# An expert's up product as seven half-size products, with the weight sums on VectorE

## The reference, cut to what matters

```python
N_EXPERTS = 8
TOP_K = 2
D_FF_EXPERT = 3584
...
    def one(args):
        xb, e = args
        return (jax.nn.silu(xb @ w_gate[e]) * (xb @ w_up[e])) @ w_down[e]
```

## Time and profile before

| what | value |
|---|---|
| median of 3 runs | 3447.71 us (3436.28 to 3449.22) |
| the profiled execution | 3443.41 us, span 3441.6 us |
| TensorE matmuls | 3270.9 us busy, 95% |
| VectorE | 895.5 us busy, 26% |
| ScalarE | 690.6 us busy, 20% |
| GpSimd | 494.8 us busy, 14% |
| mean granted TensorE clock | 0.963 of 2.4 GHz |

### The profile page before, as it was taken

One profiled execution on the slowest core, in us unless ns is written; L12 is line 12 of the kernel. 1 busy time (PEld: TensorE's weight loads), 2 busy tenths in 40 slices (PEclk: granted clock), 3 DMA queues, 4 the chain that ended last, 5 costly groups with the idle time before them and its releaser, 6 DMA issues.

```text
span 3441.6 us, 81881 instructions
## 1 busy us (share of the span) xinstructions
PE 3270.9 (95%) x35194; PEld 2864.1 (83%) x35195; DVE 895.5 (26%) x1990; ACT 690.6 (20%) x1505; POOL 494.8 (14%) x441
## 2 busy tenths in 40 slices
PE   7999789999999999999999999989999999999998
PEld 5886678888887788787799887778899999988888
DVE  2324745553223321114233114131000110011001
ACT  2324132221113422212211021201111211100011
POOL 1210125555221010100057010000000000000000
PEclk9999689999899999999999999989999999999999
DMA  6546012222233244343344443238999999944477
GB/s 275 197 165 233 3 49 86 85 85 86 74 104 110 96 149 141 128 138 107 110 160 159 158 135 109 88 132 336 376 381 400 387 395 380 399 153 147 140 274 292
DMA packets 94204, 638.90 MB, mean 186 GB/s; under 512 B 10720, under 2 KB 11760, under 8 KB 36480
## 3 DMA queue, kind: packets, MB, share of 16 engines
q1 hardware_dynamic: 91472, 628.62, 49.0%
q0 software_dynamic: 2608, 8.49, 0.8%
HBM read 636.02 MB, written 1.05 MB: 185 GB/s over the span
## 4 chain that ended last, share of the span: by engine, by line
PE 88%; DMA 4%; DVE 3%; issue 2%; ACT 2%; POOL 1%; SPq 0%; ACTq 0%; DVEq 0%; POOLq 0%
PE bank L1109 18%; PE bank L663 17%; PE bank L618 12%; PE bank L781 12%; PE bank L802 5%; PE bank L634 5%; PE bank L719 3%; PE bank L1069 2%; DMA ring<-in_moe_down 2%; PE bank L566 2%; DMA ring<-in_moe_up 1%; PE bank L592 1%; PE bank L1124 1%; PE bank L838 1%; PE bank L820 1%
## 5 line engine op out<-in xcount | busy, mean ns | idle before, releaser
L781 PE MATMUL bank<-PROJ,ring 128*64 128x80 f32 (+1 forms) x7424 | 484.6, 257 | 10.8 <-DMA ring<-in_moe_down 6.6
L1109 PE MATMUL bank<-MIX,ring 128*64 128x80 f32 x12544 | 471.9, 234 | 18.3 <-issue 7.5
L781 PEld LDWEIGHTS bank<-PROJ,ring 128*64 128x64 f32 (+1 forms) x7424 | 441.7, 145 | 52.4 <-DMA ring<-in_moe_down 11.8
L1109 PEld LDWEIGHTS bank<-MIX,ring 128*64 128x64 f32 x12544 | 447.0, 137 | 44.1 <-issue 37.0
L618 PE MATMUL bank<-H,ring 128*128 128x256 f32 x1856 | 407.3, 382 | 4.3 <-ACT H L1297 4.3
L618 PEld LDWEIGHTS bank<-H,ring 128*128 128x128 f32 x1856 | 354.3, 191 | 56.8 <-issue 4.7
L1109 PE MATMUL bank<-H,ring 128*128 128x256 f32 x896 | 195.3, 381 | 0.0
L1109 PEld LDWEIGHTS bank<-H,ring 128*128 128x128 f32 x896 | 171.3, 191 | 23.9 <-issue 0.3
L663 PE MATMUL bank<-H,ring 128*64 128x128 f32 (+1 forms) x1296 | 184.8, 330 | 5.8 <-ACT H L1297 5.1
L663 PE MATMUL bank<-MIX,ring 128*64 128x128 f32 (+1 forms) x1272 | 181.1, 321 | 0.8 <-DVE MIX L1884 0.8
L802 PE MATMUL bank<-H,ring 128*128 128x256 f32 x768 | 178.1, 390 | 3.9 <-ACT PROJ L1396 3.7
(11 more groups left out here) (383 smaller groups left out, 3716.8 us busy)
## 6 DMA issues: line engine op xcount, KB each, us to landing
ring<-in_moe_up SPq DMA_DIRECT2D x224, 1024.0 KB, 7.2
ring<-in_moe_down SPq DMA_DIRECT2D x128, 896.0 KB, 6.3
ring<-in_up SPq DMA_DIRECT2D x44, 1024.0 KB, 4.8
ring<-in_mod_b SPq DMA_DIRECT2D x40, 1024.0 KB, 4.9
ring<-in_tproj SPq DMA_DIRECT2D x32, 1024.0 KB, 4.8
ring<-in_proj SPq DMA_DIRECT2D x26, 1024.0 KB, 4.8
ring<-in_gates SPq DMA_DIRECT2D x24, 1024.0 KB, 4.8
ring<-in_swup SPq DMA_DIRECT2D x22, 1024.0 KB, 4.8
```

Source lines behind the costliest of these rows:

```text
L781: mm = pe.matmul(B[bank][lo:lo + m, 0:width], w[:, k, lo:lo + m], src(s * half + k), start=s == 0 and k == 0, stop=s == 1 and k == half - 1)
L1109: mm = pe.matmul(B[(t0 + 2 * j + t) % 4][lo:lo + m, 0:n], w[:, k, t * P + lo:t * P + lo + m], src[:, k, 0:n], start=k == 0, stop=k == KT - 1)
```

## The change

The dense branch takes `up_seven`, `gate_seven` and `expert_seven` in place of `up` and the two `swiglu`. The sparse branch keeps its code and adds to the new semaphores what the dense branch would have. The four weight sums of a unit run on VectorE; GpSimd has no part in it.

```diff
+        def e_x(b, s):
+            return H[:, 4 * b:4 * b + 4, s * P:(s + 1) * P]
+        def e_x_sum(i):
+            return MIX[:, 4 + i, :].rearrange("p (k t) -> p k t", t=P)
+        def e_parts(j):
+            at = T + P * (j % 2)
+            return X[:, 0:4, at:at + P], X[:, 4:6, at:at + P]
+        def e_banks(j):
+            b0 = 4 * (j % 2)
+            return b0, [b0 + 1 + i for i in range(3)]
...
+                def up_seven(e):
+                    with pe.Fori(0, ET // NSLOT) as it:
+                        for j in range(NSLOT):
...
+                            pe.wait_ge(S("sv_c"), e * ET + it * NSLOT + (RES_E + j - 1))
+                            if j == 1:
+                                pe.wait_ge(S("mo_wc"), e + 1)
+                            product(w_quarter(u, 0, 0), e_x(0, 0), solo, 0).then_inc(S("sv_p1"), 1)
+                            product(w_quarter(u, 0, 1), e_x(1, 0), pair[0], 0)
+                            pe.wait_ge(S("e_s"), e * ET + it * NSLOT + (j + 1))
+                            if j == 0:
+                                pe.wait_ge(S("sv_x"), e * 4 + (X_E + 4))
+                            product(w_sum(u, j, 1), e_x_sum(1), pair[0], 1).then_inc(S("sv_p"), 1)
+                            product(w_sum(u, j, 0), e_x_sum(0), pair[1], 0)
+                            product(w_sum(u, j, 2), e_x_sum(2), pair[1], 1).then_inc(S("sv_p"), 1)
+                            product(w_sum(u, j, 3), e_x(1, 1), pair[2], 0)
+                            product(w_quarter(u, 1, 1), e_x_sum(3), pair[2], 1).then_inc(unit_done, 1)
+                    pe.wait_ge(S("sv_c"), e * ET + (RES_E + ET))
...
-                        up(e, H, T)
+                        up_seven(e)
                     with pe.Else():
                         pe.sem_inc(S("mo_w"), 1)
+                        pe.sem_inc(S("sv_p1"), ET)
+                        pe.sem_inc(S("sv_p"), 2 * ET)
                         up(e, XG, CAP)
...
+            def gate_seven(e):
+                        act.wait_ge(S("sv_p1"), e * ET + it * NSLOT + (RES_E + j + 1))
+                        act.activation(part[:, 1, :], B[e_banks(j)[0]][:, 0:P], ACT.Copy).then_inc(S("sv_c0"), 1)
+                        act.wait_ge(S("sv_c"), e * ET + it * NSLOT + (RES_E + j + 1))
...
+                        act.activation(CONV[:, j % 2, 0, 0:T].rearrange("p (s t) -> p s t", t=P), d[:, 0:2, :], ACT.Silu)\
+                           .then_inc(S("sw_s"), 1)
...
+            def expert_seven(e):
...
+                def w_sums(j, it):
...
+                    dve.tensor_tensor(s2, a11, a21, ALU.subtract).then_inc(S("e_w"), 1)
...
+                    dve.tensor_tensor(s0, a21, a22, ALU.add).then_inc(S("e_w"), 1)
...
+                    dve.tensor_tensor(s1, s0, a11, ALU.subtract).then_inc(S("e_w"), 1)
...
+                    dve.tensor_tensor(s3, a12, s1, ALU.subtract).then_inc(S("e_s"), 1)
...
+                def unit(j, it, ahead):
...
+                    dve.tensor_tensor(d[:, 1:3, :], d[:, 1:3, :], both[2], ALU.add).then_inc(S("sv_c"), 1)
+                    if ahead:
+                        w_sums(j + 2, it)
+                    dve.wait_ge(S("sw_s"), e * ET + it * NSLOT + (FT + j + 1))
+                    g = CONV[:, j % 2, 0, 0:T]
+                    dve.tensor_tensor(g, g, GW[:, :], ALU.mult).then_inc(S("moe_g"), 1)
...
+                w_sums(0, 0)
+                dve.wait_ge(S("mo_xg"), e * 2 + 2)
+                dve.tensor_tensor(t1, x12, x11, ALU.subtract).then_inc(done, 1)
+                dve.tensor_tensor(t3, x22, x12, ALU.subtract).then_inc(done, 1)
+                dve.wait_ge(done, e * 4 + (X_E + 2))
+                dve.tensor_tensor(t2, x22, t1, ALU.subtract).then_inc(done, 1)
+                dve.wait_ge(done, e * 4 + (X_E + 3))
+                dve.tensor_tensor(t4, x21, t2, ALU.subtract).then_inc(done, 1)
+                w_sums(1, 0)
+                with dve.Fori(0, ET // NSLOT - 1) as it:
+                    for j in range(NSLOT):
+                        unit(j, it, True)
...
```

More of the change, by code:

```diff
@@ L472, in seven_parts @@
             return d.rearrange("p (i t) -> p i t", t=n), e.rearrange("p (i t) -> p i t", t=n)
+        RES_E = sum(4 if s in DOWNS else SEVEN_UNITS[s] for s in SEVEN)
+        X_E = sum(12 if s in DOWNS else 4 for s in SEVEN)
+        def e_x(b, s):
[8 more added lines that the diff above has]
+            return b0, [b0 + 1 + i for i in range(3)]
         def hid(width):
@@ L1111, in up, with product @@
                             mm.then_inc(unit_done, 1)
+                def up_seven(e):
+                    with pe.Fori(0, ET // NSLOT) as it:
+                        for j in range(NSLOT):
+                            u = MOE0 + j
+                            solo, pair = e_banks(j)
+                            def product(left, right, bank, half):
+                                for k in range(4):
+                                    for lo, m in strips(P):
+                                        mm = pe.matmul(B[bank][lo:lo + m, half * P:(half + 1) * P], left[:, k, lo:lo + m], right[:, k, :],
+                                                       start=k == 0, stop=k == 3)
+                                return mm
+                            pe.wait_ge(slot_full[slot_of(u)], e * (16 * PER_E // NSLOT) + it * 16 + 16 * (u // NSLOT + 1))
+                            pe.wait_ge(S("sv_c"), e * ET + it * NSLOT + (RES_E + j - 1))
[12 more added lines that the diff above has]
+                    pe.wait_ge(S("sv_c"), e * ET + (RES_E + ET))
                 def down(e, hidden, n):
@@ L1528, in swiglu @@
                     pair(j, 0)
+            def gate_seven(e):
+                t0 = tile_base["moe_up"]
+                with act.Fori(0, ET // NSLOT) as it:
+                    for j in range(NSLOT):
+                        d, part = e_parts(j)
+                        act.wait_ge(S("sv_p1"), e * ET + it * NSLOT + (RES_E + j + 1))
+                        act.activation(part[:, 1, :], B[e_banks(j)[0]][:, 0:P], ACT.Copy).then_inc(S("sv_c0"), 1)
+                        act.wait_ge(S("sv_c"), e * ET + it * NSLOT + (RES_E + j + 1))
+                        act.wait_ge(lin_free, it * (2 * NSLOT) + (t0 + 2 * j + 2) + e * (2 * ET + KT))
+                        act.activation(CONV[:, j % 2, 0, 0:T].rearrange("p (s t) -> p s t", t=P), d[:, 0:2, :], ACT.Silu)\
+                           .then_inc(S("sw_s"), 1)
             act.wait_ge(S("first_in"), 16)
@@ L1655, in _ @@
                 with act.If(dense):
-                    swiglu("moe_up", T, e)
+                    gate_seven(e)
                 with act.Else():
+                    act.sem_inc(S("sv_c0"), ET)
                     swiglu("moe_up", CAP, e)
@@ L2109, in pair @@
                     g = CONV[:, j % 2, 0, 0:width]
-                    if e is not None and width == T:
-                        dve.wait_ge(S("mo_wc"), e + 1)
-                        dve.tensor_tensor(g, g, GW[:, :], ALU.mult).then_inc(S("moe_g"), 1)
-                        dve.wait_ge(S("moe_g"), it * NSLOT + (j + 1) + es)
                     dve.tensor_tensor(PROJ[:, bass.ds(it * (NSLOT * width) + j * width, width)], g,
@@ L2249, in _ @@
                     dve.tensor_copy(GW[:, :], B[5][:, T:TC]).then_inc(S("mo_wc"), 1)
-                    swiglu("moe_up", FT, T, e)
+                    expert_seven(e)
                     add_down(MOE0 + ET, e)
@@ L2256, in _ @@
                     dve.sem_inc(S("moe_g"), ET)
+                    dve.sem_inc(S("e_w"), 3 * ET)
+                    dve.sem_inc(S("e_s"), ET)
+                    dve.sem_inc(S("sv_x"), 4)
+                    dve.sem_inc(S("sv_k"), 3 * ET)
+                    dve.sem_inc(S("sv_c"), ET)
                     for i in range(4):
```

34 lines of the change are left out of this document (added).

## The result

| | before | after |
|---|---|---|
| median of the runs, us | 3445.53 (3436.28 to 3449.22, 4 runs) | 3546.27 (3536.25 to 3552.25, 4 runs) |
| profiled run: span, us | 3441.6 | 3544.2 |
| mean granted clock of TensorE | 0.963 | 0.948 |

The ratio is 1.0287, with a 95% interval of 1.0272 to 1.0301: **slower by 2.9%**, where 0.5% faster was forecast. The forecast case had half of the chance and slower 7%.

What follows compares the result with a forecast made beforehand. The prediction took TensorE to bound the dense up product, the stage changed. Its terms, -21.4 + 3.7 + 0.7 + 0.1 = -16.9 us, gave 3426.5 from the profiled run and 3430.8 from the median; forecast 3429 us, range 3418 to 3440.

Steps and rivals of the forecast that it cites:

- The forecast case: Whole kernel: the prediction's own case, 16.9 us saved and 3429 us forecast, given a 50% chance.
- The dense up product: TensorE's stage in the dense expert: units fall from 6.907 to 6.114 us, saving 21.4 us; whole product 177.5 us.
- first unit: Start of dense up product: TensorE stands 2.8 us for VectorE's sums, then runs at half clock; 3.7 us lost.
- The gathering's 0.7 us wait: End of dense up product: TensorE waits for unit 28's last addition before gathering; 0.7 us lost.
- the predicted sum: Whole kernel: all gains and losses together, -16.9 us.
- VectorE just covered: Dense up product: VectorE's work per unit takes 5.9 us against TensorE's 6.11 us, 96% busy, so it stays hidden.
- rivals on VectorE: Dense up product: VectorE just the bound, 3440 us, 20%; or its sums slow and the kernel slower, 3465 us, 5%.
- on the clock: First dense unit: clock is up again after the stall, 1.75 us less lost, -18.6 us, 3427 us; 22%.
- on the strips: Dense up product: two strips of 64 weight columns do not run side by side, 145 us more, 3590 us; 1%.
- The seven sparse experts: Sparse turns: two more semaphore increments each on TensorE, put at 0.1 us in all, with no gain possible.
- The stage "that DMA bounds": Sparse up product: the weight stream bounds it, DMA share 0.98, so it absorbs the added semaphore increments.
- Sparse experts should keep their lengths: Sparse turns: a sign to check in the new trace, that their lengths stay unchanged.

Runs made afterwards that it cites:

- swap: The change with TensorE's sparse-turn code first in one piece and the dense turn behind it, nothing taken out: 3439.76 us, ratio 0.9984 to before.
- swapb: The kernel before, without the change, with TensorE's sparse-turn code first and the dense turn behind it: 3451.89 us, ratio 1.0008.
- up1: The kernel before with one loop turn of the dense up product written out, 1,907 instructions, nothing new computed: 3534.19 us.
- pad40: The kernel before with 40 idle products (results overwritten unread) in the dense branch, 1,802 instructions: 3460.21 us.

## Why the prediction was wrong

**The dense up product: right.** Unit 6.11 us (predicted 6.114). One stall of 2.40 us (2.8), then low clock until about 3116; first unit from 3105.89 to 3118.00, 12.1 us (12.45 from the same steps). Whole product 177.3 us (177.5). The gathering's 0.7 us wait was hidden by the fetch in the change; in swap it is 0.60 us. With the code in reach, the dense turn gave 15.8 + 1.1 = 16.9 us, the predicted sum. That it is met so exactly is luck in part: the new order alone took 1.7 us off the dense turn (295.7 for 297.4 in swapb), and against swapb it is 14.1 + 1.1 = 15.2 us.

**VectorE just covered: right.** Its instructions in one unit after the change:

```profile
3155.23 0.69 DVE L2201 TENSOR_TENSOR VT<-ring 128x512 f32<-128x512 f32 x1
3155.95 0.69 DVE L2203 TENSOR_TENSOR ring<-ring 128x512 f32<-128x512 f32 x1
...
3158.01 0.42 DVE L2230 TENSOR_TENSOR SC<-SC,GW 128x256 f32<-128x256 f32 x1
...
3159.22 0.29 DVE L2215 TENSOR_TENSOR X<-X,bank 128x128 f32<-128x128 f32 x1 [0.21 <-PE bank L1143]
...
3161.01 0.42 DVE L2225 TENSOR_TENSOR X<-X,bank 128x256 f32<-128x256 f32 x1 [0.63 <-PE bank L1143]
```

Sums of 0.69 us with gaps of 0.03 to 0.04, as taken from the earlier trace rows. The idle 0.63 us before the last addition, with the 0.21 before the first, is the room that is left; the sum of 5.9 us had put it at 0.2 us. The rivals on VectorE, on the clock and on the strips did not occur.

**The seven sparse experts: the step that failed.** "I put 0.1 us. They can gain nothing." I had priced what the change *executes* in a sparse turn, two semaphore increments, and not what it adds to the *code* that the turn runs through or jumps over. Measured: +98.6 us (88.4 and 10.2). The stage "that DMA bounds", which was to absorb a wait, did not absorb these: the turn grew by their full length and by the low clock behind them. In the dense turn the same cause took 6.1 us ahead of the gathering, 8.7 at the loop's head, and 5.8 us of low clock in the gathering and the down product (3.6 and 2.2), which no term had. No rival held this mechanism either, so the range had nothing on that side. The one number by which the prediction was to be judged, a dense up product of 175 to 180 us, came true (177.3) while the kernel lost 100 us; the sign that failed was "Sparse experts should keep their lengths".

**What could have been read.** The kernel before has a queue of instruction packets (94 of them) on its page, and in its first turn, when the code is new, TensorE waits for "issue" in the same two sparse products where it later does in every turn of the change:

```profile
2332.32 15.71 PE L1109 MATMUL bank<-MIX,ring 128*64 128x80 f32 x384 [2.59 <-issue]
...
2410.98 4.64 PE L781 MATMUL bank<-PROJ,ring 128*64 128x80 f32 x127 [0.77 <-issue]
```

With the code on the core the first of these is 0.59 us, in the turn of 2674, and the second is gone. The change lengthens the body by 39%, which the order of the instructions shows. The Trainium skill, "Runtime: NRT & Kernel Launch", section Instruction fetch mechanics, states TensorE's store as 2,048 instructions, filled in blocks of 256 and fetched ahead in sequence only, and warns of a stall at a taken branch whose target is not there. Packets of 16.4 KB, the 127 records from stall to stall in up1, and the waits at jumps (5.25 us) agree. By that page 2,284 instructions do not fit, which would have made a rival that ends on the slow side. The same section also speaks of a memory of only two blocks; for TensorE the runs disagree, as the seven blocks of pad40, or seven and a little over, came round without a fetch.

## What to carry to other kernels

Where a loop's body holds several branches, count the instructions of each engine in it, fp32 products at four each and transposes at two, before adding to one branch: the others can come to pay in every turn. Here the step came between 1,802 and 1,842 instructions of TensorE (1,791 and 1,831 in the recount) and cost 12 to 16 us a sparse turn. What decided was the number of blocks that a turn needs, not the length of the whole body; laying the frequent branch in one piece from the loop's head took the cost away with all the code still there. "issue" waits at the same lines in each turn, together with more packets on the instruction queue, are its sign.

## What the runs showed that I had not expected

- The step is sharp: 40 instructions, 4 to 6 us of work, moved the time by 110 us (one run each; before's own runs spread over 13 us).
- A wait for code at a jump was 3.1 to 8.7 us in the change, and 3.34 us even at a block's edge inside the down product; what follows runs at the low clock, 3.8 us in a sparse turn that stalled three times.
- With 80 moving columns, two strips of 64 weight columns are faster than one piece of 128: four units take 9.2 us, and 10.6 with two of their eight tiles in one piece. With 128 moving columns the strips gave 2% (6.11 for 6.25 us a unit).
- 35 products of only 8 moving columns took 14.3 us, 0.41 us each.
